# Recurrence groups moved and joined on TensorE, eight small products left out, the first weights in halves, a fourth accumulator bank, and dummy products in the entry

## The reference

```python
h = rmsnorm(x, w_norm_pre)
q_a, k_a, v_a, z_a, q_r, f_r, i_r, z_r = split(h @ w_in)          # 1024 -> 3328
o_a = sliding_window_sink_attention(rope(q_a), rope(k_a), v_a, sinks) * silu(z_a)
# recurrence, per head, chunks of 64 tokens
f = lb + (1 - lb) * sigmoid(f_r);  kk = 1 - f;  G = cumsum(log f, in the chunk)
q_dec, k_dec = q * exp(G), kk * exp(-G)
A = where(causal, q_dec @ k_dec.T, 0);   o_intra = A @ v
U = (kk * exp(G_last - G)).T @ v
S_prev = state before the chunk;  state = exp(G_last) * S_prev + U # S starts at zero
o = o_intra + q_dec @ S_prev
o_r = rmsnorm(o, hgrn_norm) * silu(z_r)
x + rmsnorm(concat(o_a, o_r) @ w_out, w_norm_post)
```

## Time and profile before

| | before |
|---|---|
| median of 3 runs | 900.52 us (900.42 to 900.83) |
| the profiled execution, its own time | 901.49 us |
| its span | 899.7 us |
| PE busy | 886.0 us, 98% of the span |
| weight loads busy | 722.9 us |
| DVE, ACT, POOL busy | 531.7, 421.6, 111.3 us |
| mean DMA rate | 207 GB/s |

### The profile page before, as it was taken

The page is one execution under the profiler, slowest core; times in us unless marked ns, Lnnn a source line. Parts: engine busy times, 40 slices in busy tenths (PEclk is TensorE's granted clock), DMA queues, the critical chain, the costliest instruction groups (busy, mean ns, idle before and its releaser), DMA issues.

```text
span 899.7 us, 12351 instructions
## 1 busy us (share of the span) xinstructions
PE 886.0 (98%) x4744; PEld 722.9 (80%) x4744; DVE 531.7 (59%) x861; ACT 421.6 (47%) x734; POOL 111.3 (12%) x90
## 2 busy tenths in 40 slices
PE   8999999999999999999999999999999999999997
PEld 6787778778888777888888878888888877788886
DVE  6678977674655775664254677556425367754523
ACT  7666456563454434544234444454423543434322
POOL 0000013320200001241020000142001000012102
PEclk9999999999999999999999999999999999999999
DMA  8686755539957644453776644444378534344463
GB/s 310 227 276 227 244 205 204 209 141 349 396 201 269 257 152 141 153 179 126 275 293 220 230 167 140 154 158 166 136 283 327 187 143 160 119 152 176 141 239 135
DMA packets 52634, 186.03 MB, mean 207 GB/s; under 512 B 5856, under 2 KB 6112, under 8 KB 52576
## 3 DMA queue, kind: packets, MB, share of 16 engines
q1 hardware_dynamic: 49840, 178.29, 55.4%
q10 hardware_dynamic: 2736, 6.95, 1.9%
HBM read 141.18 MB, written 44.04 MB: 206 GB/s over the span
## 4 chain that ended last, share of the span: by engine, by line
PE 92%; issue 3%; ACT 2%; DVE 2%; DMA 1%; POOL 0%; SPq 0%; DVEq 0%; ACTq 0%; POOLq 0%
PE bank L428 59%; PE bank L437 10%; PE score_b L437 5%; PE turn_b L437 5%; PE turn_b L479 2%; PE bank L505 2%; PE score_b L457 2%; PE bank L513 2%; PE bank L522 1%; PE bank L520 1%; PE score_b L501 1%; PE turn_b L469 1%; ACT w_hi L650 1%; DMA x_in<-in_x 1%; PE score_b L529 0%
## 5 line engine op out<-in xcount | busy, mean ns | idle before, releaser
L428 PE MATMUL bank<-h_lo,w_hi 128*128 128x512 f32 x832 | 330.0, 397 | 0.0
L428 PE MATMUL bank<-h_hi,w_hi 128*128 128x512 f32 x832 | 329.2, 397 | 0.8 <-ACT h_hi L687 0.5
L428 PE MATMUL bank<-h_hi,w_lo 128*128 128x512 f32 x832 | 327.8, 394 | 0.0
L428 PEld LDWEIGHTS bank<-h_lo,w_hi 128*128 128x128 f32 x832 | 157.1, 189 | 37.9 <-issue 6.4
L428 PEld LDWEIGHTS bank<-h_hi,w_hi 128*128 128x128 f32 x832 | 157.4, 189 | 34.3 <-issue 2.0
L428 PEld LDWEIGHTS bank<-h_hi,w_lo 128*128 128x128 f32 x832 | 157.2, 189 | 34.2 <-issue 0.7
L1152 POOL TENSOR_TENSOR mix_lo<-v_r,mix_hi 128x512 fp32r<-128x512 f32 x16 | 20.6, 1290 | 527.9 <-ACT v_r L789 527.9
L856 DVE TENSOR_TENSOR w_lo<-w_raw,w_hi 128x1024 fp32r<-128x1024 f32 x37 | 44.9, 1221 | 34.8 <-ACT w_hi L650 34.8
L654 ACT ACTIVATE g_a<-g_b 128x512 f32<-128x512 f32 x32 | 20.2, 631 | 75.3 <-DVE g_b L920 75.3
L650 ACT ACTIVATE w_hi<-w_raw 128x1024 fp32r<-128x1024 f32 x40 | 41.8, 1050 | 21.2 <-DMA kept_lo<-w_lo 8.0
L437 PE MATMUL bank<-w_lo,mix_hi 128*128 128x512 f32 x128 | 50.1, 392 | 0.0
(11 more groups left out here) (160 smaller groups left out, 1412.8 us busy)
## 6 DMA issues: line engine op xcount, KB each, us to landing
w_hi<-kept_hi SPq DMA_DIRECT2D x96, 512.0 KB, 3.7
w_lo<-kept_lo SPq DMA_DIRECT2D x96, 512.0 KB, 4.6
w_raw<-in_weights SPq DMA_DIRECT2D x40, 512.0 KB, 5.5
kept_hi<-w_hi SPq DMA_DIRECT2D x34, 512.0 KB, 5.7
kept_lo<-w_lo SPq DMA_DIRECT2D x34, 512.0 KB, 7.1
x_in<-in_x_rows SPq DMA_DIRECT2D x8, 1024.0 KB, 7.6
x_in<-in_x SPq DMA_DIRECT2D x15, 512.0 KB, 6.6
out<-q_gate ACTq DMA_DIRECT2D x9, 512.0 KB, 9.2
```

The costliest lines, as they stand in the source:

```text
L428: mm = pe.matmul(acc(w)[:, :], stationary[:, s, k, :], moving[:, k, :], start=(m == 0), stop=(m == 3 * KT - 1), skip_group_check=True)
```

## The change

The arithmetic is the same but for products whose result is zero or is never used.

1. `head_out(h)` goes from gate(h) + 2, m = 8 to gate(h + 1), m = 12, directly ahead of `head_scores(h + 1)`; for the last head to gate(h) + 2, m = 16. `head_states(h)` goes to gate(h) + 1, m = 16, behind `head_sum(h - 1)`; for head 0 to m = 20, behind `weigh`.
2. The output goes to `out_b` (half of turn_b) instead of head_b, queries alternate between two buffers, pair states lie in `probs` instead of in h_mix. `carry_head` is two steps later and stands ahead of k_mid; the output gating, mixing and the low parts are one or two steps later.
3. In token tile 0 the state product of the first pair is left out, and the scaling of the empty state; in token tile 3 the fourth U of each head and the last state.
4. The first two weight tiles are loaded, split and waited for in halves; the squares of x are added two slices at a time; `sum_x` goes to m = 16 in token tile 0.
5. Accumulators are bank[w % 4] up to w = 11.
6. Six dummy products instead of eight ahead of the entry, one ahead of slice 1 and two ahead of slice 2 of w = 0.
7. Attention's gating and the copy of turned probabilities stand earlier in their steps; weight splits of the next token tile's first step go ahead of the output transfers on ACT.

The diff, cut to what matters:

```diff
+def out_step(h):
+    return gate(h) + (4 if h < HEADS - 1 else 2)
...
+FILL = {1: 1, 2: 2}
...
+        q_even, k_mid = sb("q_even", [N]), sb("k_mid", [N])
+        q_mid = (q_even, v_t)
...
-        pair_state = h_mix[:, :].rearrange("p (q n) -> p q n", q=PAIRS)
+        pair_state = probs[:, 0:PAIRS, :]
...
+        out_b = turn_b[:, 1, :]
...
-            return bank[w % 3]
+            return bank[w % 4 if w <= query(0) else w % 3]
...
+        def state_pairs(t):
+            return PAIRS if t + 1 < TILES else PAIRS - 1
...
             sp.dma_start(x_in[:, 0, :], x[0:P, 0:N]).then_inc(x_head, 16)
-            load_raw(0)
+            load_half(K_TILE, 0)
             sp.dma_start(x_in[:, 1, :], x[0:P, N:2 * N]).then_inc(x_quarter[0], 16)
-            for k in range(2, KT, 2):
-                if k == 4:
-                    load_raw(1)
+            load_first_x(2)
+            load_half(V_TILE, 0)
+            load_half(K_TILE, 1)
+            load_first_x(4)
+            load_half(V_TILE, 1)
+            load_first_x(6)
...
-                pe.wait_ge(o_rstd.sem, o_rstd.after(t, h - 1))
+                pe.wait_ge(o_rstd.sem, o_rstd.after(t, h - 2))
                 (transposes)
-                pe.wait_ge(o_gated.sem, o_gated.after(t, h - 1))
+                if t + 1 < TILES or h == 0:
+                    pe.wait_ge(carried.sem, carried.after(t, h - 1))
+                else:
+                    pe.wait_ge(state_done.sem, state_done.after(t, h - 1))
                 (four products A)
...
             def head_states(t, h):
-                for p in range(PAIRS):
+                for p in range(state_pairs(t)):
...
             def head_out(t, h):
                 pe.wait_ge(state_done.sem, state_done.after(t, h))
+                pe.wait_ge(o_gated.sem, o_gated.after(t, h - 1))
                 for p in range(PAIRS):
-                    pe.matmul(head_b[:, pair(p)], kv_tok[:, 1, pair(p)], a_t[:, pair(p)], ...)
-                    mm = pe.matmul(head_b[:, pair(p)], read_state[:, p, :], q_mid[:, pair(p)], ...)
+                    empty = t == 0 and p == 0
+                    mm = pe.matmul(out_b[:, pair(p)], kv_tok[:, 1, pair(p)], a_t[:, pair(p)], ...)
+                    if not empty:
+                        mm = pe.matmul(out_b[:, pair(p)], read_state[:, p, :], q_mid[h % 2][:, pair(p)], ...)
...
-                if w == XSUM and m == (0 if t else 8):
+                if w == XSUM and m == (0 if t else 16):
...
                 for h in range(HEADS):
+                    if w == out_step(h) and m == (12 if h < HEADS - 1 else 16):
+                        head_out(t, h)
                     if w == gate(h) and m == 12:
                         head_scores(t, h)
-                    if w == gate(h) + 1 and m == 8:
+                    if h and w == gate(h) + 1 and m == 16:
                         head_states(t, h)
-                    if w == gate(h) + 2 and m == 8:
-                        head_out(t, h)
-                    if w == gate(h) + 3 and m == 18:
+                    if w == out_step(h) + 1 and m == (16 if h < HEADS - 1 else 18):
                         head_sum(t, h)
                 (weigh)
+                if w == gate(0) + 1 and m == 20:
+                    head_states(t, 0)
...
-            for i in range(8):
+            for i in range(6):
                 pe.matmul(head_b[:, 0:P], ones, ones, start=True, stop=True)
...
+                        if w == K_TILE and part == 0:
+                            for i in range(FILL.get(k, 0)):
+                                pe.matmul(head_b[:, 0:P], ones, ones, start=True, stop=True)
...
             def carry_head(t, h):
-                dve.wait_ge(mixh_lo.sem, mixh_lo.after(t, h - 1))
+                dve.wait_ge(turned.sem, turned.after(t, PAIRS - 1))
...
+                    for h in range(HEADS):
+                        if s == out_step(h) - 1 and h < HEADS - 1:
+                            carry_head(t, h)
                     if kind == 1:
                         (k_mid, f_d)
                     if kind == 3:
                         gate_first(t, QT + h_of)
-                        carry_head(t, h_of)
...
-                        if s == gate(head) + 4:
+                        if s == out_step(head) + 2:
                             (ACT: mix_hi of the head)
```

160 lines of the change are left out of this document (99 added, 61 removed).

## The result

The changed kernel takes 892.05 us at the median of its first four runs (891.13 to 893.87), against 900.47 for the kernel before beside it: a ratio of 0.9917, 95% interval 0.9905 to 0.993. The prediction was 892.0. The change is worth 7.0 us, and not the 8.4 of the first pair: two terms of my sum were too large and two too small, and the first four runs drew an early entry, so that the first median comes within 0.05 us of 892.0 is luck. The rest of the text shows which terms.

A forecast was written before the change was run, and what follows sets the result against it. PE, busy 98% of the span, was taken as the bound, with 11.6 us to win from waits and clock, all in tile 0. Savings of 1.8 + 0 + 5.6 + 1.1 = 8.5 us gave 892.0 us, range 888.5 to 896.8.

The forecast's parts named there:

- Products left out: Output groups of tile 0 and state products of tile 3: eight products at 0.223 us each save 1.8 us.
- Joins: Output and U groups placed beside transposes, weigh or sum products: saving taken as 0, bounds 0 and 5.5 us.
- the rival that joins save: At 16 joined places, a quarter to all of a pause saved, 1.4 to 5.5 us: 887 to 890.5; chance 0.12.
- Waits of tile 0: Behind tile 0's sum over x: waits and slow clock shrink, saving 5.6 us, bounds 3.5 and 6.9.
- The lost 7.3 us: PE time lost behind tile 0's sum over x: tile 0 takes 226.1 us for what later tiles do in 218.8.
- the 1.84: PE's 1.84 us wait at the scores of head 3 in tile 0, followed by a group at the lower clock.
- The chain that I added up to 15.2 to 15.5 us: DVE and ACT work in tile 0 from f_b to v_r, predicted 0.2 to 0.5 us late for the transposes.
- Entry: Ahead of tile 0's sum over x: dummies in the gaps raise the clock sooner, 1.1 us; half tiles give 0.
- The later sum over x: Tile 0's sum comes 1.8 us later, delaying key rotation; ACT's slack and the fourth bank cover it, cost 0.
- Sum: Whole kernel: 1.8 + 0 + 5.6 + 1.1 = 8.5 us saved, 892.0 at the median.
- Waits move on: Rival: tile 0's heads 2 and 3 wait as before, only 1 to 3 us remain: 894.5 to 897.5; chance 0.20.
- Slower by v_r late in tiles 1 to 3: Rival: carry_head ahead of k_mid makes v_r 1.1 us late, costing 10.2 us: about 902; chance 0.04.

The follow-up runs named there:

- the split behind v_r: Changed kernel, but in tile 0 VectorE makes the low weight half of the step before each v_r behind v_r and to_next; median 891.04 us.
- the variant of before: Kernel before with only the pair states of heads 1 to 3 moved from h_mix to probs; median 898.55 us, ratio 0.9981.
- the last experiment: Changed kernel with four unused 512-column reductions on VectorE ahead of every v_r in tiles 1 to 3; 900.46 us, ratio 1.0005 to the kernel before.

## Why the prediction was right in its total, point by point

**Products left out** (1.8 forecast). 0.84 in tile 3 and 0.87 in tile 0 by themselves: right. But 1.25 more in tile 0 belong to the same edit, since the scaling of the empty state went with the product, and beside POOL it held VectorE for 1.3 us at heads 1, 2 and 3, so that f_b of the next head started late. I had the mechanism in hand for g_mid and for the states and did not apply it to an instruction that the change removes. The edit measured 2.96.

**Joins** (0, bounds 0 and 5.5). 0.59 over the four tiles. The value taken was nearest, and the rival that joins save is out. The rule cited from the Trainium skill, TensorEngine Tiling (Array Packing), section Key Properties, that a change of mode drains the engine, gives 0, and the trace agrees within 0.02 us a join; the saving of the earlier trace rows was seen only between two groups of the same shape. (16 x 0.35 is 5.6, not the 5.5 of the bound.)

**Waits of tile 0** (5.6, bounds 3.5 and 6.9). The lost 7.3 us became 216.40 + 16 x 0.227 - 218.67 + 0.87 = 2.2, so 5.1 went, of which 1.25 by the removed scaling above and 1.5 are the lower clock behind the 1.84. Left were 0.77 each at heads 2 and 3 (0.5 forecast) and 0.44 at weigh. The chain that I added up to 15.2 to 15.5 us takes 15.7 (134.38 to 150.10) and ended 0.7 late; DVE was full, and the split behind v_r shows that nothing else held PE. That it was not later is owed to the removed scaling, which the sum did not have: with it the waits are 1.08 and 1.58. What the moved groups took away by themselves is the wait at the output (0.87 with what follows), those at the squares and at U of head 0, and little at the transposes; no run has them alone, nor item 7 of the change. My statement that a wait of 0.99 leaves the clock up and one of 1.84 drops it is wrong as a rule: 1.85 left it up in the variant of before, and 11 of 42 runs of before itself have no room for a drop. The clock did stay up in both traces of the changed kernel, as forecast.

**Entry** (1.1, bounds 0 and 2.4). This step failed. The measured worth is -0.24, between -0.6 and 0.1, from 49 runs. I took slice 2 to come no later with half the weight tile ahead of it, and gave dummies a share of the clock. Slice 2 came 0.8 us later at the median, and the dummies gave 1.7 to 2.0 us (26.55 and 26.41 against 24.58 and 24.67) only against the halves without them. That the 3.78 us of dummies did not raise the clock was so in the profiled execution of before; in its variant the products are 0.24 us apart from 8.1 on, soon after the same eight dummies. And that the first sum over x starts near the 24.9 that I gave (24.67 at the mean) is luck: the profiled execution of before, from which I counted, has that sum at 24.16 + 1.81 = 25.97, a late one. The sentence cited from the Trainium skill, TensorE: Matmul & The Clock Gate, section What's actually happening, that the rise of the clock is not tied to the kernel's start, would have made this term 0, and was nearer; the traces agree, in that the first rise comes anywhere between 6 and 12 us behind the same six dummies.

**The later sum over x** (0, covered by the fourth bank). Right, and shown by taking the cover away: 2.1 us.

**Sum.** 8.5 forecast; 2.96 + 0.59 + 3.82 = 7.37 behind the first sum over x (3.82 is what is left of 6.09 in tile 0 after 2.12 and 0.16), less 0.24 in the entry: 7.1, and the 9 and 42 runs show 7.0 (899.69 - 892.67). The 7.37 go by the one trace of before; in the runs of before without the fall of the clock they are 1.5 less. The sum was 1.4 us too large: 1.3 too much in the entry and 1.8 in the waits, 1.2 and 0.6 too little in products and joins. That it came so near the total is errors that cancel. 900.5 - 8.5 was forecast, 899.7 - 7.0 measured; the rest is that the median of before was 0.8 us lower over many runs.

**Rivals.** Waits move on: no, they went, except for 1.5 us of them. Slower by v_r late in tiles 1 to 3: no wait there at all, and by the last experiment 1.6 us of spare time at the tightest heads; I had feared 0.1 to 1.1 late, because I counted the states' 2.0 to 3.0 us on top and too little of what left the chain.

## What to carry to other kernels

When an edit removes a product from the bottleneck engine, list the instructions of the other engines that existed for it, and read what each costs at its place and not alone: in tile 0 they were worth more than the products (1.25 against 0.87 us). Work that is due only steps later (a weight split) must not stand ahead of the one result that the bottleneck engine waits for next; one such move gave 1.8 us for three lines. And a gain in a start-up phase should be believed only over dozens of runs: subtract the distances behind a landmark from every run's span, and the phase can be compared without more profiles, if the mean clock of each run says that the distances are those of the trace.

## What the runs showed of the hardware that I had not expected

- A 128x128 scaling on VectorE takes 0.28 us alone and 1.33, 1.32 and 1.32 us when a GpSimd subtraction of 128x512 began just before it: it ends with GpSimd's instruction. Still smaller ones are held as well: a 128x3 product of two SBUF tiles (to_next) takes 0.15 us at head 3 and 1.25 us at head 2 of the changed kernel, where GpSimd was busy.
- After nearly the same idle time of PE (1.84 and 1.85 us) at the same place of nearly the same program, the granted clock fell to 0.50 in the trace of one kernel and stayed at 1.00 in that of the other, and by the mean clocks of the runs both kernels do both.
- Transfers cut in halves brought the first weights to PE 1.3 us sooner (first product at 5.67 to 5.93 in nine traces, against 6.93 to 7.17 in five) and the next slice of x 0.8 us later at the median.
- With the same entry code the start of the sum over x differs by 3.4 us between 35 runs (22.94 to 26.38), while in the traces the distances behind it repeat to 0.1 us.
